# Output projection of a hybrid encoder layer: one pass over all tokens, or two passes over half of them with the first gate and up products behind

## The chip, the cores and the metric

One of the cores of a Trainium2 chip runs the whole program. The metric is the device time of one execution in microseconds. The engines in what follows are TensorE (PE, matmuls), VectorE (DVE), ScalarE (ACT), GpSimd (POOL) and SyncE (SP, which issues most of the DMAs). Each engine works through its own queue in order; they wait for each other through semaphores.

## What is computed

One layer for 560 tokens in float32: 16 meta tokens, 512 prompt tokens and 32 tokens of a running stream. The meta tokens are only keys and values: from the output projection on, 544 tokens count, in two halves of 272.

```python
def layer(h, attend, conv_state, w_in, w_out, conv_w, ...):
    proj = jnp.einsum('btd,de->bte', rms_norm(h, g_pre_mix), w_in)
    q, k, v, gate_b, gate_c, conv_in = jnp.split(proj, SPLITS, axis=-1)
    attn = attend(q, k, v).reshape(b, t, ATTN_WIDTH)
    conv_y, conv_last = short_conv(gate_c * conv_in, conv_state, conv_w)
    mix = jnp.concatenate([group_rms_norm(attn, ...), group_rms_norm(gate_b * conv_y, ...)], axis=-1)
    h = h + rms_norm(jnp.einsum('bte,ed->btd', mix, w_out), g_post_mix)
    xf = rms_norm(h, g_pre_ffn)
    ff = jax.nn.silu(jnp.einsum('btd,df->btf', xf, w_gate)) * jnp.einsum('btd,df->btf', xf, w_up)
    return h + rms_norm(jnp.einsum('btf,fd->btd', ff, w_down), g_post_ffn), k, v, conv_last
```

d_model is 2048 (16 chunks of 128), d_ff 5632 (44 chunks).

## The kernel before

Activations lie with features on the 128 partitions and tokens on the columns. Every float32 operand of a matmul is split into a rounded high part and the low rest, and each product is three matmuls: high x high, high x low, low x high. So a tile of weights is loaded by a DMA, then ACT casts the high part, then DVE subtracts it to get the low part, and then PE can use it.

In the input and the output projection a tile is 8 k-chunks x 128 columns (512 KB). It is loaded into one of two raw buffers (`w_raw`, `load`, L526) and split into one of four slots of `w_hi` and `w_lo` (`round_weights`, L412; `rest_of_weights`, L420). The load of tile t waits until tile t-2 is split; the cast of tile t waits until PE has used tile t-4. Two tiles make the 128 outputs of a chunk. In the output projection there are 16 such chunks, each over all 544 tokens (`two_chunks`, L911, for the first two, which start while the last mix chunks are still being made; `chunk`, L648, for the rest). ACT squares a finished chunk, DVE evacuates it with a gain (L1754), POOL adds up the squares. The loads stand in SP's queue: eight tiles, then waits for the stores of the mixing stage, then the load of the whole residual (4.48 MB, L585), then the other tiles.

When all 16 chunks are there, PE sums the squares over the partitions with matmuls (`row_sums`, L709), ACT makes rstd from them (Ln, Exp, each with its table), DVE scales and adds to the residual (L1763 to L1772), ACT squares the result, PE sums again (L937), ACT makes the second rstd, and DVE normalizes (`normalize`, L1802).

Gate and up projection use a Strassen-like scheme over 2 x 2 blocks: tokens in halves, the contraction in halves of 8 chunks, outputs in pairs of chunks. A step (44 of them, gate and up in turn) has seven products instead of eight, in the order B11, B21, T2, T3, T1, T4, B22 for the weights (`combine`, L1781, makes T1 to T4 on DVE) with A11, A12, S2, S3, S1, A22, S4 for the activations (`xs`; A11 and A12 belong to the first half of the tokens, S1 to S4 are sums and differences of blocks of both halves, made on DVE at L1827 to L1830 and L1914). A product is 8 x 3 = 24 matmuls of 272 columns (`product`, L948). Weights come in panels of 1 MB (`load_panel`, L589); a ring of four tiles (`t_hi`, `t_lo`) holds the split ones. `x_rest` (L1797) splits the activations. The down projection follows with 24 steps of the same kind.

Of the kernel before, what the change touches and what calls it, by code (L numbers as in the profile page):

```python
# [25 lines left out]
P = 128  # L26
# [3 lines left out]
def build_layer(nc, x_prompt, x_sample, cache_k, cache_v, state_conv, meta, w_in, w_out, conv_w,  # L30
# [26 lines left out]
    TK = 8  # L57
# [4 lines left out]
    OUT_T = 2 * KC  # L62
    CH_OUT = IN_T // 2
    CH_FF = CH_OUT + KC
# [56 lines left out]
    with ExitStack() as ctx:  # L121
# [58 lines left out]
        xs = sb_at("xs", 0, [P, 7, 2, KH, TH], F32R)  # L180
# [8 lines left out]
        h2_sq = sb_at("h2_sq", 35840, [P, KC, TL])  # L189
# [5 lines left out]
        hid_hi = sb_at("hid_hi", 201408, [P, 7, TH], F32R)  # L195
        HID_OF = {A11: 1, A12: 2, S2: 5, S3: 0, S1: 4, A22: 3, S4: 6}
# [123 lines left out]
        mix_hi = sem("mix_hi")  # L320
        mix_split = [sem("mix_split0"), sem("mix_split1")]
# [4 lines left out]
        h2_squared = sem("h2_squared")  # L326
        x_normed = sem("x_normed")
# [127 lines left out]

        def panel_of(step, half):
# [29 lines left out]
        def raw_tile(i):  # L486

            step, q = i // 7, i % 7
# [5 lines left out]
        def tile_of(ring, i):  # L494
            return in_tile(ring[:, i % RING_T, :], i // 7)
# [16 lines left out]
        def _(sp):  # L512
# [58 lines left out]
            def load_out(q):  # L571
                at_col = q * 2 * P
                for k in range(4):
                    load((4, q, T_OUT), k, w_out_v[:, TK * (k % 2):TK * (k % 2 + 1),
                                                   bass.ds(at_col + k // 2 * P, P)])
# [10 lines left out]
            for q in range(2, KC // 2):  # L586
                load_out(q)

# [23 lines left out]
            for step in range(1, ALL):  # L612
                if step == 2:
                    sp.wait_ge(xs_lo, 8)
                if step > 2:
                    sp.wait_ge(tile_lo, 7 * (step - 1))
                if step == 1:
                    sp.wait_ge(tile_lo, T1 + 1)
                load_panel(step, 0)
                if step == 1:  # L620
                    sp.wait_ge(xs_lo, 8)
                else:
                    sp.wait_ge(tile_lo, 7 * (step - 1) + T1 + 1)
# [20 lines left out]
        def _(pe):  # L644
# [266 lines left out]
            def two_chunks(tile0, x_wait, lag, between):  # L911


                for c in range(KC + lag):
                    for j, k in ((0, c), (1, c - lag)):
                        if not 0 <= k < KC:
                            continue
                        if k % TK == 0:
                            pe.wait_ge(lo_ready, tile0 + 2 * j + k // TK + 1)
                        if j == 0:  # L920
                            pe.wait_ge(*x_wait(c))
                        mm = multiply(2 * j + k // TK, TK, P, 0, act_hi, act_lo, k // TK * TK, acc_late[j],
                                      [k % TK], k < TK, k >= TK)
                        if k % TK == TK - 1:
                            mm.then_inc((first_used, chunk_done)[k // TK], 1)
                    if c in between:
                        between[c]()

            pe.wait_ge(chunk_copied, CH_OUT)
            two_chunks(T_OUT, mix_chunk, 2, {6: last_norm_and_rows})  # L930
            for q in range(1, KC // 2):
                for c in range(2):
                    chunk((4, q, T_OUT), 2 * c, 2 * q + CH_OUT + c, no_points)
            row_sums(sq_added, sq_made, buf_g[:, LATE], squares[(KC - 1) % 2])


            for g in range(KC // 2):  # L937
                pe.wait_ge(h2_squared, g + 1)
# [1155 lines left out]
```

## Time and profile before

| | us |
|---|---|
| median of three runs | 2453.63 (2452.96 to 2456.07) |
| the profiled execution, its own time | 2450.74 |
| its span in the profile | 2449.0 |
| output projection on PE, steady part | 766 to 934 |
| from its end to the steady gate and up products | 934 to 1022 |

The profile has one execution. Its page gives each engine's busy time and share. [...] The chain of waits is followed back from the last instruction and read forward here: when a piece starts, how long it is, whose it is. Rows of a timeline have start, length, engine, line, operation, output and input, shape, and in brackets how long the engine had been idle and what ended that. Rows of groups have the total and mean length, then the idle time before them. Rows of DMA issues have the count, the size of each, and the median time from issue to landing.

### The profile page before, as it was taken

To read this page: it belongs to the slowest core of one execution; us is meant where nothing else is said; L and a number is where in the kernel's file an instruction comes from. 1 tells how busy PE (TensorE), PEld (TensorE's weight loads), DVE (VectorE), ACT (ScalarE), POOL (GpSimd) and SP (SyncE) were. 2 spreads that over 40 slices of the span, in tenths; PEclk is the share of its full clock that TensorE was granted. 3 is DMA by queue.
4 is the path that set the end of the run, shared out by engine and by line. 5 is a ranking of instruction groups with operands and counts; after the bars stand their busy time and mean duration, and the time that the engine had idled before them with its cause. 6 is when DMAs were issued, how large, how long until landed. Compare 5 with 4: busy or idle time off the path is not lost.

```text
span 2449.0 us, 42232 instructions
## 1 busy us (share of the span) xinstructions
PE 2374.5 (97%) x18280; PEld 2334.6 (95%) x18280; DVE 1541.6 (63%) x1778; ACT 1011.0 (41%) x1245; POOL 81.9 (3%) x143
## 2 busy tenths in 40 slices
PE   8999999999999996699999999999999899999998
PEld 7999999999999995699999999999999899999998
DVE  5323333343434225877777777777777688888887
ACT  6345444432333223444444444444444333333346
POOL 0000000000002110000000000000000000000002
PEclk9999999999999998799999999999999999999999
DMA  7222322222324331234445444444445666645562
GB/s 234 84 75 70 97 77 79 74 87 87 87 81 146 99 104 73 75 130 133 154 135 168 136 154 149 132 155 134 154 134 168 246 210 231 231 143 156 183 204 87
DMA packets 325916, 327.93 MB, mean 134 GB/s; under 512 B 8508, under 2 KB 282324, under 8 KB 325604
## 3 DMA queue, kind: packets, MB, share of 16 engines
q1 hardware_dynamic: 299264, 275.57, 35.9%
q10 hardware_dynamic: 26468, 49.67, 5.5%
q8 instruction: 145, 2.38, 0.4%
q14 instruction: 39, 0.32, 0.0%
HBM read 264.20 MB, written 61.00 MB: 133 GB/s over the span
## 4 chain that ended last, share of the span: by engine, by line
PE 90%; DVE 5%; DMA 2%; ACT 2%; issue 1%; SPq 0%; POOL 0%; ACTq 0%; DVEq 0%; POOLq 0%
PE ps L955 37%; PE ps L438 30%; PE ps L1012 17%; PE ps L722 4%; DMA ff_lo_scr<-hid_lo 2%; PE ps L666 1%; DVE xs L1800 1%; DVE t_lo L1778 1%; DVE misc L1804 0%; DVE panel L1792 0%; DVE wide L1768 0%; DVE misc L1772 0%; ACT xs L1350 0%; DMA panel<-in_w_down_dram 0%; DMA misc<-in_x_sample_dram 0%
## 5 line engine op out<-in xcount | busy, mean ns | idle before, releaser
L955 PE MATMUL ps<-xs,t_hi 128*128 128x272 f32 x4928 | 940.6, 291 | 33.0 <-DVE xs L1800 19.1
L955 PEld LDWEIGHTS ps<-xs,t_hi 128*128 128x128 f32 x4928 | 781.1, 190 | 34.6 <-issue 32.2
L955 PE MATMUL ps<-xs,t_lo 128*128 128x272 f32 x2464 | 716.8, 291 | 0.0
L1778 DVE TENSOR_TENSOR t_lo<-panel,t_hi 128x1024 fp32r<-128x1024 f32 (+1 forms) x405 | 485.5, 1199 | 228.3 <-ACT t_hi L1343 225.3
L1343 ACT CAST t_hi<-panel 128x1024 fp32r<-128x1024 f32 (+1 forms) x405 | 413.4, 1021 | 455.1 <-PE ps L1012 241.9
L1012 PE MATMUL ps<-xd,t_hi 128*128 128x272 f32 x2464 | 470.4, 290 | 14.3 <-DVE y_left L1949 8.2
L955 PEld LDWEIGHTS ps<-xs,t_lo 128*128 128x128 f32 x2464 | 467.3, 190 | 0.0
L438 PE MATMUL ps<-act_hi,w_hi 128*128 128x272 f32 (+1 forms) x2048 | 435.4, 294 | 3.1 <-DVE act_lo L1615 1.9
L438 PE MATMUL ps<-act_lo,w_hi 128*128 128x272 f32 (+1 forms) x2048 | 426.9, 290 | 0.0
L438 PE MATMUL ps<-act_hi,w_lo 128*128 128x272 f32 (+1 forms) x2048 | 426.5, 289 | 0.0
L1012 PEld LDWEIGHTS ps<-xd,t_hi 128*128 128x128 f32 x2464 | 390.7, 190 | 15.5 <-issue 15.4
L1012 PE MATMUL ps<-xd,t_lo 128*128 128x272 f32 x1232 | 358.3, 291 | 0.0
L438 PEld LDWEIGHTS ps<-act_hi,w_hi 128*128 128x128 f32 x2048 | 322.8, 189 | 7.1 <-DVE act_lo L1615 2.6
L438 PEld LDWEIGHTS ps<-act_hi,w_lo 128*128 128x128 f32 x2048 | 324.2, 189 | 0.0
L438 PEld LDWEIGHTS ps<-act_lo,w_hi 128*128 128x128 f32 x2048 | 323.9, 189 | 0.0
L424 DVE TENSOR_TENSOR w_lo<-w_raw,w_hi 128x1024 fp32r<-128x1024 f32 x126 | 157.9, 1254 | 194.8 <-ACT w_hi L418 194.1
L418 ACT CAST w_hi<-w_raw 128x1024 fp32r<-128x1024 f32 x128 | 133.7, 1046 | 281.1 <-PE ps L438 222.4
L1012 PEld LDWEIGHTS ps<-xd,t_lo 128*128 128x128 f32 x1232 | 233.5, 190 | 0.0
L1343 ACT CAST t_hi<-t_raw 128x1024 fp32r<-128x1024 f32 (+1 forms) x68 | 69.7, 1025 | 112.6 <-PE ps L955 69.4
L1381 ACT ACTIVATE m<-ps 128x272 f32<-128x272 f32 x88 | 35.2, 400 | 149.0 <-PE ps L955 149.0
L1549 DVE TENSOR_TENSOR misc<-misc 128x1440 f32<-128x1440 f32 x8 | 13.3, 1658 | 114.3 <-ACT misc L1126 114.3
L1792 DVE TENSOR_TENSOR t_raw<-panel,panel 128x1024 f32<-128x1024 f32 (+1 forms) x67 | 79.3, 1183 | 8.4 <-DMA panel<-in_w_down_dram 6.1
(183 smaller groups left out, 1728.4 us busy)
## 6 DMA issues: line engine op xcount, KB each, us to landing
w_raw<-in_w_in_dram SPq DMA_DIRECT2D x96, 512.0 KB, 3.8
panel<-in_w_up_dram SPq DMA_DIRECT2D x44, 1024.0 KB, 5.6
panel<-in_w_gate_dram SPq DMA_DIRECT2D x43, 1024.0 KB, 5.1
panel<-in_w_down_dram SPq DMA_DIRECT2D x32, 1024.0 KB, 5.9
ff_hi_scr<-hid_hi SPq DMA_DIRECT2D x22, 952.0 KB, 4.5
ff_lo_scr<-hid_lo SPq DMA_DIRECT2D x22, 952.0 KB, 7.4
w_raw<-in_w_out_dram SPq DMA_DIRECT2D x32, 512.0 KB, 3.9
xd<-ff_hi_scr ACTq DMA_DIRECT2D x28, 544.0 KB, 8.0
```

What stands on the lines that cost most here:

```text
L418: nc.scalar.copy(w_hi[:, k % SLOTS, :], raw_slot(k)).then_inc(hi_ready, 1)
L424: engine.tensor_tensor(w_lo[:, k % SLOTS, :], raw_slot(k), w_hi[:, k % SLOTS, :].bitcast(F32), ALU.subtract).then_inc(lo_ready, 1)
L438: mm = nc.tensor.matmul(out[:, h, :], w[:, k, col:col + width], x[:, x_at + k, token + h * half:token + (h + 1) * half], start=begins, sto ...
L666: return nc.tensor.transpose(out, src, ident[0:n, 0:n])
L722: return nc.tensor.matmul(out, w, x, start=start, stop=True, skip_group_check=True)
L955: mm = nc.tensor.matmul(out, w[:, k, :], xs[:, x, part, k, :], start=begins and k == 0 and w is hi and part == 0, stop=k == KH - 1 and w i ...
L1012: mm = nc.tensor.matmul(out[:, n, :], w[:, k, n * P:(n + 1) * P], xd[:, slot, part, k, :], start=q in (B11, B21, T3) and k == 0 and w is h ...
L1343: nc.scalar.copy(tile_of(t_hi, i), raw_tile(i)).then_inc(tile_hi, 1)
L1381: A(out[step % 2][:, :], step_bank(step, letter), ACT.Copy).then_inc(made, 1)
L1778: V.tensor_tensor(tile_of(t_lo, i), raw_tile(i), tile_of(t_hi, i).bitcast(F32), ALU.subtract)\
L1792: V.tensor_tensor(out, x, y, ALU.subtract).then_inc(t_made, 1)
L1800: V.tensor_tensor(xs[:, x, 1, k:k + n, :], block, xs[:, x, 0, k:k + n, :].bitcast(F32), ALU.subtract) .then_inc(xs_lo, 1)
```

## The change

The output projection runs in two passes: first all 16 chunks of outputs for the first half of the tokens, then again for the second half. So a block (the code's e, 0 to 31) is one chunk for 272 tokens, two tiles with 24 matmuls each, and every w_out tile is loaded, cast and split twice. The mix is split into separate tiles for the halves (`mx_hi`, `mx_lo`). Four more tiles, the first ones of gate (two) and up (two), follow through the same raw buffers; PE makes the products B11 and B21 of steps 0 and 1 from them (`pre_product`) behind the second pass, between the sums of the second half's squares. The stage's tail for the first half (scale, add, squares, second rstd, normalization, splits of A11 and A12) is put between the blocks of the second pass on DVE and ACT; its squares are folded on DVE, for one matmul behind block 24. The tail of the second half comes behind the last block, and the sums S1 and S2 get tiles of their own. The stores of the residual go from SP's to ACT's queue.

```diff
-    OUT_T = 2 * KC
+    OUT_T = 4 * KC + 4
...
+        PRE = 4
...
+        def ring(step, q):
+            return 7 * step + q - (2 if step == 0 else PRE)
...
             sp.dma_start(resid, h_scr).then_inc(h_loaded, 16)
-            for q in range(2, KC // 2):
+            for q in range(2, KC):
                 load_out(q)
+            for k in range(PRE):
+                load((4, KC, T_OUT), k, gate_up[k // 2][:, TK * (k % 2):TK * (k % 2 + 1), 0:P])
...
-            for g in range(KC // 2):
-                sp.wait_ge(h2_made, g + 1)
-                sp.dma_start(h_scr[:, 2 * g:2 * g + 2, LATE], resid[:, 2 * g:2 * g + 2, LATE])                  .then_inc(h2_stored, 16)
-
...
+            for e in range(2, 2 * KC):
+                if e >= 4:
+                    pe.wait_ge(out_copied, e - 3)
+                if e == KC:
+                    pe.wait_ge(mix_late, 4)
+                for half in range(2):
+                    pe.wait_ge(lo_ready, T_OUT + 2 * e + half + 1)
+                    out_part(e, half, list(range(TK)))
+                if e == KC:
+                    out_sums(0)
+                if e == KC + 8:
+                    pe.wait_ge(h2_summed, 4)
+                    nc.tensor.matmul(ps[:, 5, 0:TH], neg1[:, :], h2_sq[0][:, 0, :], start=True, stop=True)\
+                        .then_inc(ms_ready, 1)
+            out_sums(1)
...
+            pe.wait_ge(ms_log, 3)
+            pre_product(0)
+            pre_product(1)
+            h2_sums(0)
+            pre_product(2)
+            for g in range(1, 4):
+                h2_sums(g)
+            pre_product(3)
...
+            def square_stream(t, g):
+
+                act.wait_ge(h2_made, 4 * t + g + 1)
+                h = x_block(4 * g, 4, t)
+                A(h2_sq[t][:, 4 * g:4 * g + 4, :], h, ACT.Square).then_inc(h2_squared, 1)
+                act.dma_start(h_scr[:, 4 * g:4 * g + 4, tokens_of(t)], h).then_inc(h2_stored, 16)
+
             act.wait_ge(mixed, end)
...
+            for e in range(2 * KC):
+                t, n, q = e // KC, e % KC, e // 2
+                for half in range(2):
+                    ahead = 2 * e + half + LEAD
+                    if 2 * e + half >= 2 and ahead < OUT_T:
+                        round_weights((4, ahead // 4, T_OUT), ahead % 4)
...
+                A(squares[n % 2][:, t * TH:(t + 1) * TH], ps[:, n % 4, 0:TH], ACT.Square).then_inc(sq_made, 1)
+                if e == KC:
+                    make_rstd(1)
+                if e in (KC + 4, KC + 6):
+                    for g in range(2):
+                        square_stream(0, e - KC - 4 + g)
+                if e == KC + 9:
+                    make_rstd(2)
...
+            for ahead in range(4 * KC + LEAD, OUT_T):
+                round_weights((4, ahead // 4, T_OUT), ahead % 4)
...
+            make_rstd(3)
+            for g in range(4):
+                square_stream(1, g)
+            load_log_table(2)
+            tile_high(ring(0, T2))
+            make_rstd(4)
+            act.wait_ge(product_done, PRE)
+            x_high(A22, x_block(KH, KH, 1), x_normed, 8)
+            x_high(S2, s2_raw[:, :, :], s_made, 2)
...
+            for e in range(2 * KC):
+                t, n = e // KC, e % KC
+                for half in range(2):
+                    ahead = 2 * e + half + LEAD
+                    if 2 * e + half >= 2 and ahead < OUT_T:
+                        rest_of_weights((4, ahead // 4, T_OUT), ahead % 4)
+                if e in (4, 6, 8, 10):
+                    mix_rest_late((e - 4) // 2)
+                dve.wait_ge(sq_made, e + 1)
+                V.tensor_scalar(wide_c[:, n, tokens_of(t)], ps[:, n % 4, 0:TH], column(n + C_POSTMIX), None, ALU.mult)\
+                    .then_inc(out_copied, 1)
+                if e in (KC + 1, KC + 2):
+                    for g in range(2):
+                        scale_mix(0, 2 * (e - KC - 1) + g)
+                if e in (KC + 3, KC + 5):
+                    for g in range(2):
+                        add_mix(0, e - KC - 3 + g)
+                if e == KC + 7:
+                    fold_squares(0)
+                if e == KC + 8:
+                    for level in range(1, 4):
+                        fold_squares(level)
+                if e == KC + 10:
+                    dve.wait_ge(rstd_ready, 3)
+                    dve.wait_ge(h2_stored, 16 * 4)
+                    normalize(0, 0, 4)
+                    normalize(0, 4, 4)
...
-            tile_rest(B11)
+            for g in range(-1, 4):
+                if g + 1 < 4:
+                    scale_mix(1, g + 1)
+                if g >= 0:
+                    add_mix(1, g)
             combine(0, T1)
             combine(0, T2)
             combine(0, T3)
...
+            V.tensor_tensor(s1_raw[:, :, :], a21, a22, ALU.add).then_inc(s_made, 1)
+            dve.wait_ge(product_done, PRE)
+            dve.wait_ge(s_made, 1)
+            V.tensor_tensor(s2_raw[:, :, :], s1_raw[:, :, :], a11, ALU.subtract).then_inc(s_made, 1)
             x_rest(A22, 4, a22)
-            V.tensor_tensor(a22, a21, a22, ALU.add).then_inc(s_made, 1)
             V.tensor_tensor(a21, a11, a21, ALU.subtract).then_inc(s_made, 1)
...
+            x_rest(S2, 5, s2_raw[:, :, :])
+            V.tensor_tensor(a12, a12, s2_raw[:, :, :], ALU.subtract).then_inc(s_made, 1)
```

## Rows read from the trace of the kernel before

**Rows 1.** The page, span and busy time of each engine.
```profile
span 2449.0 us, 42232 instructions
PE 2374.5 (97%) x18280; PEld 2334.6 (95%) x18280; DVE 1541.6 (63%) x1778; ACT 1011.0 (41%) x1245; POOL 81.9 (3%) x143
```
**Rows 2.** The table by stage: out projection, transition, first gate and up steps.
```profile
766.00:934.00 168.00, 168.00 (x1343) 168.00 (x1342) 47.09 (x41) 35.47 (x42) 20.93 (x14) 1.00 0.38 119
934.00:1022.00 88.00, 47.31 (x223) 41.11 (x222) 73.16 (x60) 38.75 (x36) 0.00 (x0) 0.75 0.19 70
1022.00:1140.00 118.00, 118.00 (x925) 118.00 (x925) 90.14 (x101) 54.96 (x71) 0.00 (x0) 0.99 0.42 136
```
**Rows 3.** The chain of waits: start, length, piece.
```profile
934.57 1.91 PE ps L716 x8
...
1001.36 1.14 DVE t_lo L1778
...
1021.78 88.25 PE ps L955 x686
```
**Rows 4.** Groups of PE from 934 to 1022, the gate and up products.
```profile
L955 PE MATMUL ps<-xs,t_hi 128*128 128x272 f32 x98 | 25.7, 361 | 33.0 <-DVE xs L1800 19.1 <-ACT m L1381 11.9 <-DVE gate L1850 2.0
...
L955 PE MATMUL ps<-xs,t_lo 128*128 128x272 f32 x48 | 16.9, 352 | 0.0
```
**Rows 5.** Timeline of ACT: casts of raw tiles, both buffers.
```profile
784.87 1.05 ACT L418 CAST w_hi<-w_raw 128x1024 fp32r<-128x1024 f32 x1 [13.03 <-DMA w_raw<-in_w_out_dram]
...
786.34 1.05 ACT L418 CAST w_hi<-w_raw 128x1024 fp32r<-128x1024 f32 x1
791.16 1.05 ACT L418 CAST w_hi<-w_raw 128x1024 fp32r<-128x1024 f32 x1 [3.77 <-DMA w_raw<-in_w_out_dram]
...
793.97 1.05 ACT L418 CAST w_hi<-w_raw 128x1024 fp32r<-128x1024 f32 x1 [1.24 <-DMA w_raw<-in_w_out_dram]
```
**Rows 6.** Timeline of DVE: last mix chunk's split, a raw tile's split.
```profile
757.43 0.73 DVE L1731 TENSOR_TENSOR act_lo<-wide,act_hi 128x544 fp32r<-128x544 f32 x1 [0.77 <-ACT act_hi L1292]
...
785.96 1.23 DVE L424 TENSOR_TENSOR w_lo<-w_raw,w_hi 128x1024 fp32r<-128x1024 f32 x1 [12.86 <-ACT w_hi L418]
```
**Rows 7.** Timeline of SP's queue: loads of tiles and of the residual.
```profile
766.88 0.37 SPq L531 DMA_DIRECT2D w_raw<-in_w_out_dram  x1
767.68 0.34 SPq L585 DMA_DIRECT2D misc<-h_scratch  x1
768.07 0.42 SPq L531 DMA_DIRECT2D w_raw<-in_w_out_dram  x1
...
787.21 0.37 SPq L531 DMA_DIRECT2D w_raw<-in_w_out_dram  x1
```
**Rows 8.** DMA issues: count, size, median time to landing.
```profile
w_raw<-in_w_out_dram SPq DMA_DIRECT2D x32, 512.0 KB, 3.9
...
misc<-h_scratch SPq DMA_DIRECT2D x1, 4480.0 KB, 15.4
```
**Rows 9.** Timeline of PE behind a gap: pairs of matmuls.
```profile
1002.20 0.79 PE L955 MATMUL ps<-xs,t_hi 128*128 128x272 f32 x2 [9.63 <-ACT m L1381]
...
1008.42 0.41 PE L955 MATMUL ps<-xs,t_hi 128*128 128x272 f32 x2
```
**Rows 10.** Groups of DVE from 934 to 1022, by shape.
```profile
L1804 DVE SCALAR_TENSOR_TENSOR misc<-misc,cols,rstd 128x544 f32<-128x544 f32 x16 | 11.4, 776 | 0.0
L1768 DVE TENSOR_TENSOR wide<-wide,rstd 128x1088 f32<-128x1088 f32 x8 | 10.2, 1284 | 3.2 <-ACT rstd L1094 3.2
...
L1827 DVE TENSOR_TENSOR misc<-misc 128x2176 f32<-128x2176 f32 x1 | 2.4, 2418 | 0.0
```
**Rows 11.** Groups of ACT from 934 to 1022.
```profile
L1331 ACT ACTIVATE h_sq<-misc 128x1088 f32<-128x1088 f32 x8 | 8.9, 1111 | 11.6 <-DVE misc L1772 11.5
...
L1094 ACT ACT_TABLE_LOAD x2 | 2.6, 1283 | 0.0
...
L1087 ACT ACTIVATE rstd<-ps,eps 128x544 f32<-128x544 f32 x2 | 1.4, 714 | 1.6 <-PE ps L716 1.3 <-PE ps L943 0.4
```

More of the change, by code:

```diff
@@ L929, in _ @@
-            pe.wait_ge(chunk_copied, CH_OUT)
[L930 to L938, printed above, removed]
-                for c in (2 * g, 2 * g + 1):
-                    for h, bank in enumerate((bank_a, bank_b)):
-                        if c == 0:
-                            pe.wait_ge(ms_log, 2)
-                        mm = nc.tensor.matmul(bank[:, 0:TH], neg1[:, :], h2_sq[:, c, h * TH:(h + 1) * TH],
-                                              start=c == 0, stop=c == KC - 1)
@@ new lines, in out_sums @@
+            def out_sums(t):
+                for part, (x, added_up) in enumerate(((buf_g[:, tokens_of(t)], (sq_added, (KC - 1) * (t + 1))),
+                                                      (squares[(KC - 1) % 2][:, t * TH:(t + 1) * TH],
+                                                       (sq_made, KC * (t + 1))))):
+                    pe.wait_ge(*added_up)
+                    mm = nc.tensor.matmul(ps[:, 4 + 2 * t, 0:TH], neg1[:, :], x, start=part == 0, stop=part == 1)
+                mm.then_inc(ms_ready, 1)
@@ new lines, in _, with pre_product @@
+            out_sums(1)
+            def pre_product(k):
+                step, q = k // 2, k % 2
+                pe.wait_ge(lo_ready, T_OUT + 4 * KC + k + 1)
+                pe.wait_ge(xs_lo, 3 if q else 2)
+                pe.wait_ge(out_copied, 2 * KC)
+                hi, lo = (w[:, k, :].rearrange("p (k n) -> p k n", k=TK) for w in (w_hi, w_lo))
+                for c in range(KH):
+                    for w, part in ((hi, 0), (hi, 1), (lo, 0)):
+                        mm = nc.tensor.matmul(step_bank(step, "ac"[q]), w[:, c, :], xs[q][:, part, c, :],
+                                              start=c == 0 and w is hi and part == 0, stop=c == KH - 1 and w is lo,
+                                              skip_group_check=True)
+                mm.then_inc(product_done, 1)
@@ new lines, in normalize, with x_rest @@
+            def normalize(t, c0, n):
+                for c in range(c0, c0 + n):
+                    x = resid[:, c, tokens_of(t)]
+                    last = V.scalar_tensor_tensor(out=x, in0=x, scalar=column(c + C_PREFFN), in1=rstd[:, tokens_of(t)],
+                                                  op0=ALU.mult, op1=ALU.mult)
+                last.then_inc(x_normed, 1)
+            def x_rest(x, made, block, k=0, n=KH):
+                dve.wait_ge(xs_hi, made)
+                V.tensor_tensor(xs[x][:, 1, k:k + n, :], block, xs[x][:, 0, k:k + n, :].bitcast(F32), ALU.subtract)\
+                    .then_inc(xs_lo, 1)
@@ L1775, in tile_rest @@
+            for ahead in range(4 * KC + LEAD, OUT_T):
+                rest_of_weights((4, ahead // 4, T_OUT), ahead % 4)
             def tile_rest(i):
@@ L1954, in _ @@
                 step = STEPS + d
-                ahead = 7 * (step + 1)
                 more = step + 1 < ALL
```

373 lines of the change are left out of this document (197 added, 176 removed).

## The prediction

> **What bounds the kernel now.** I read first the busy shares of the page [rows 1]: TensorE (PE) is busy 97% of 2449.0 us, so only its gaps and its pace can give time. Then the table by stage [rows 2]. In the out projection (766 to 934 us) PE is busy in all of 168.00 us with 1343 matmuls: 0.125 us each, so a weight tile of 24 matmuls on 272 columns is 3.00 us. From 934 to 1022 it is busy 47 of 88 us at a granted clock of 0.75, while VectorE (DVE) is busy 73: that is the stage to win in, and it is a DVE chain. The chain of waits says the same: matmul sums at 934.57, then nearly only DVE and ScalarE (ACT) until 1021.78, from where PE runs on [rows 3]. Up to 1022 PE had run 146 matmuls of the gate/up products [rows 4], two of them after 1021.78: 144, or six products. At 24 x 0.126 us a product is worth 3.02 us; so if PE had begun at 1003.7 without a gap it would stand at the same place. After that it still lost some 2 us to pace (925 matmuls in 118.00 us, where 0.125 each is 115.7 [rows 2]). So today's stage works like a clean start at 1005.7, 71 us after the out projection's end at 934.5.
>
> **What the change does to the weights.** Each w_out tile (512 KB) is loaded, cast and split twice, once per half of the tokens: 64 tiles and four gate/up tiles where there were 32. PE's matmuls stay 1536; a tile feeds 24 of them where it fed 48. So PE asks for a tile every 3.00 us, not every 6.0. A tile goes through one of two raw buffers, and the next load into that buffer waits for the split. One round of a buffer stands in the trace where PE was not the limit: cast at 784.87 and again at 791.16 [rows 5], 6.29 us a round: 1.09 from cast to split [rows 6], 1.25 from split to the next load's issue [rows 7], 3.95 from issue to the cast. Two buffers give a tile per 3.15 us. That is more than 3.00: today the buffers have nearly half of PE's time to spare, after the change they set the pace. The other buffer's round there was 7.63 (786.34 to 793.97 [rows 5]), with an evacuation between: I take 6.29, and 6.00 (PE's own pace) and 7.6 are the bounds.
> [...] The trace's median for these loads, issued from SyncE (SP), is 3.9 us [rows 8], and I go by it.
>
> **Start of the first pass.** The load of the residual (4.48 MB, 15.4 us [rows 8]) stands in SP's queue behind the first eight tiles. The tile load behind it, issued at 768.07 [rows 7], could be cast only at 784.87, after a wait of 13.03 [rows 5]: 16.8 us after issue. Today PE has four tiles of 6 us in hand and does not notice. In the new order the first two blocks end some 1.5 us after the last mix chunk is split (757.43 [rows 6], a little earlier with half the width): 758.8. ACT can round tile 5 only behind the square of block 0: cast, split, the next load at 761.3, the residual's load 0.8 later and tile 8's at 762.5, with the spacing of [rows 7]. It is usable at 762.5 + 16.8 + 1.1 + 1.2 = 781.6. PE ran out of tiles at 758.8 + 12.0 = 770.8: **a stall of 10.8 us**. [...]
>
> **The two passes.** From tile 8 the even buffer gives tile 48 after 20 rounds: 781.6 + 125.8 = 907.4. The odd buffer follows 2.8 us later at first. DVE and ACT get more work between its rounds as of block 16: scale and add on 1088 columns (1.28 us each, 1.20 apart), two 1.11 us squares and two store issues on ACT, table loads of 1.28 [rows 10, 11]. A round leaves DVE 6.3 - 2 x 1.2 - 0.4 = 3.4 us, so pieces of 2.4 fit once the odd tiles have slid to some 4.6 us behind the even ones. With 0.8 us for the stores: tile 49 at 912.7 and block 24 (0 is the first) done at 915.7.
> **The fold.** Behind block 24 PE's queue has a wait for four sums of squares that DVE folds, and three of its four folds come after block 24's own evacuation. ACT must first round tiles 51 and 52 (tile 52 lands at 918.8), so: cast to 919.9, square, split of 52 to 921.1, evacuation to 921.5, folds of 1088, 544 and 272 columns 2.6 us, one matmul: 924.4. **PE stands 8.7 us**, and every tile behind it in PE's queue stands too. If ACT were ahead it would be 3.7 (square 0.4, evacuation 0.4, folds 2.6, matmul 0.3). [...]
> Fourteen tiles of 3.00 follow: **the out projection ends at 924.4 + 2.5 + 42.0 = 968.9, 34.4 us later than today**.
>
> **The new transition.** The last gate/up tile's load is issued when tile 65 is split (970.1) and lands at 974.1; its cast on ACT stands ahead of the second half's rstd: 1.05, Ln 0.4, table 1.28, Exp 0.4 (half of [rows 11]): R = 977.2. From R: eight half operations of 1.2 (9.7); the last square, its store's issue, a table load with its activation, the cast of T2's tile and the second rstd on ACT: R + 16.2; 16 normalizations of 272 columns, 0.41 each (0.78 on 544 with 0.70 apart [rows 10], half plus the fixed part): R + 22.9; two sums of 2176 (2.35 apart) and then three more such operations, the last the split of S2: T2 of step 0 starts at R + 34.7. From the split of S2 to the last product of step 0 it takes 20.4 us today (1001.36 to 1021.78 [rows 3]), now 19.2, since the split of step 1's first tile is gone; four more DVE operations to T2 of step 1: R + 57.9 = 1035.1. By then nine products are done, four of them early (27.2 us), in PE time that DVE's chain leaves free anyway. The clean start is at 1007.9.
> **Sum:** 1007.9 against 1005.7 is +2.2 us: the stage itself falls from 71 to 39 us and gives 32, and the passes take 34.4 of it back. The profiled execution took 2450.74 us (span 2449.0); the median of three is 2453.63, and I add to that: **2456 us**. The four early products, half 0's norm and the panel loads behind SP's queue (5 us each, landing before R) are costed at nothing because DVE's chain covers them. Should the early products find no cover, they cost 12 us. The steps and the down projection keep their order and lengths.
>
> **The rivals.**
> A, the forecast: 2456, itself 2451 to 2462 by the steps' own slack (the fold's wait, the odd buffer's slide, half pace).
> B, PE sets the pace: a load lands in 3.6 us or less and rounds run ahead. Then block 24 ends at 781.6 + 2.8 + 126 = 910.4, the fold costs 3.7 and 1.5 of pace, the end is 957.6, and R comes 3.7 us after it, since tile 67 is there: clean start at 992.0, 13.7 us faster: 2440. For it: rows of 3.9 are only 0.3 us from the point where 6.29 turns to 6.00. Against it: that 6.29 is what the row shows where nothing else held the buffer.
> C, the slower side: DVE's and ACT's inserted work pushes both buffers' rounds, not the odd one's alone. The place is blocks 16 to 30, and it decides as soon as an insertion is over the 3.4 us that a round leaves. With a mean round of 7.0 us, halfway to 7.63, it is 15 x 0.7 = 10.5 us: 2466. For it: the row of 7.63, with one evacuation alone. Against it: that round caught up at once.
> D, the change doesn't do what it says: half 0's norm is not through by the end of pass two and the early products come behind the DVE chain, 12 us: 2468.
>
> **How the numbers follow.** A 0.46, B 0.25, C 0.20, D 0.09. About 0.2% (4.9 us) is what a measurement here can tell from no change: 2448.7 to 2458.5. A lies in it with 0.33 and above it with 0.13; B below with 0.24 and 0.01 inside; C above with 0.18 and 0.02 inside; D above. So faster 0.24, same 0.36, slower 0.40. A alone is the likeliest and it crosses the bound. The range goes from just above B's time to just above D's: 2441 to 2469.
>
> **What would show it.** In the profile after: PE without work for some 11 us near 771 to 782, with the cast of tile 8 waiting for a DMA; ACT's casts of w_raw waiting for the DMA and not for PE, with 6.3 us between every second one; a wait of 4 to 9 us of PE for DVE some 50 us ahead of the out projection's end; that end near 969; T2 of step 0 some 43 us after it. I am wrong if the casts wait for PE (B), if rounds in pass two are 7 us (C), or if the end of the projection is before 958.

## The result: slower by 13.8 us, with the profile after

| | before | after |
|---|---|---|
| median of the timed runs | 2453.63 us (2452.96 to 2456.07) | 2467.40 us (2466.70 to 2469.87) |
| ratio to before, 95% interval | | 1.0058 [1.0046, 1.0069] |
| the profiled execution, its span | 2450.74, 2449.0 | 2467.40, 2465.7 |

The forecast was 2456 in 2441 to 2469: the time is in the range, 11.4 us above the forecast, and on the side that had the chance 0.40.

The page of after, against [rows 1]: PE has the same busy time, so the loss is in gaps again.

```profile
span 2465.7 us, 42439 instructions
PE 2374.8 (96%) x18250; PEld 2332.2 (95%) x18250; DVE 1587.8 (64%) x1851; ACT 1051.7 (43%) x1306; POOL 96.0 (4%) x158
```

The table by stage of after, with the stretches of [rows 2] (the stretch and its length; busy us, and in brackets the instructions, of PE, PE's weight loads, DVE, ACT, POOL; PE's granted clock as a share of full speed, DMA share, GB/s):

```profile
766.00:934.00 168.00, 140.28 (x1045) 135.22 (x1044) 87.97 (x86) 66.41 (x82) 29.97 (x22) 0.94 0.60 172
934.00:1022.00 88.00, 63.75 (x452) 61.22 (x452) 66.59 (x74) 44.89 (x49) 8.29 (x6) 0.88 0.40 122
1022.00:1140.00 118.00, 113.25 (x859) 112.46 (x859) 92.63 (x98) 55.11 (x70) 0.00 (x0) 0.96 0.40 132
```

Of the first 168 us PE now lacks 27.7, where it lacked none. In the middle stretch it has 452 matmuls instead of 223, but a part of these are the out projection, which ends there. In the last it has 859 against 925. The clean start of the sum (where PE would have to begin gate and up without a gap) is found as before: step 1's block T2, from which PE runs on, begins at 1044.71, and nine products of 3.02 us stand ahead of it: 1017.5. For before, six products ahead of 1021.78 give 1003.7. The difference is 13.8 us, as much as that of the medians.

The two profiled executions differ by 16.7 us. The other 3 are at the end of the program, which the change does not touch: the same 177 matmuls had a granted clock of 1.00 in before's execution and 0.86 in after's. In an execution of the kernel before with one more buffer (an experiment below) it was 0.81. So I put it down to the execution, not to the change; one execution of each kernel was profiled. The three rows are before, after, and that kernel:

```profile
2426.00:2449.00 23.00, 19.36 (x177) 18.64 (x176) 14.32 (x20) 13.75 (x24) 0.00 (x0) 1.00 0.55 195
```
```profile
2439.40:2465.70 26.30, 22.54 (x177) 21.62 (x176) 14.78 (x20) 13.98 (x24) 0.00 (x0) 0.86 0.47 171
```
```profile
2425.00:2452.00 27.00, 24.11 (x177) 23.17 (x177) 14.77 (x20) 14.15 (x24) 0.00 (x0) 0.81 0.46 166
```

Now the stage itself, in three places. The DMA issues of after, to set beside [rows 8]:

```profile
w_raw<-in_w_out_dram SPq DMA_DIRECT2D x64, 512.0 KB, 4.0
...
misc<-h_scratch SPq DMA_DIRECT2D x1, 4480.0 KB, 15.1
```

**The passes.** ACT's timeline of after, the casts of raw tiles behind the start (in brackets: idle before it, and what ended it), to set beside [rows 5]:

```profile
773.62 1.04 ACT L429 CAST w_hi<-w_raw 128x1024 fp32r<-128x1024 f32 x1 [11.56 <-DMA w_raw<-in_w_out_dram]
...
787.11 1.05 ACT L429 CAST w_hi<-w_raw 128x1024 fp32r<-128x1024 f32 x1 [3.67 <-DMA w_raw<-in_w_out_dram]
```

The line of these casts in after from 782 to 918 us, as a group:

```profile
L429 ACT CAST w_hi<-w_raw x40: 1035/1048/1059, 782.4 to 917.0; 128x1024 fp32r<-128x1024 f32 x40
...
  DMA w_raw<-in_w_out_dram: 77.9, 38
```

The same line in before, from 766 to 934 us:

```profile
L418 ACT CAST w_hi<-w_raw x26: 1040/1047/1052, 765.5 to 911.1; 128x1024 fp32r<-128x1024 f32 x26
...
  PE ps L438: 40.5, 9
  DMA w_raw<-in_w_out_dram: 24.2, 5
```

In before 9 of the 26 casts waited for PE and 5 for a load; after the change 38 of 40 wait for a load, and none is put down to PE. 40 casts from 782.4 to 917.0 are 39 steps of 3.45 us: PE gets a tile every 3.45 us, where it can use one every 3.00. From PE's side, its timeline around the stall at tile 8, 9.7 us from the start of one matmul to the start of the next:

```profile
766.36 0.28 PE L947 MATMUL ps<-mx_hi,w_lo 128*128 128x272 f32 x1
776.07 0.57 PE L947 MATMUL ps<-mx_hi,w_hi 128*128 128x272 f32 x1 [9.42 <-DVE w_lo L435]
```

**The fold.** The chain of waits of after around it (start, length, piece):

```profile
909.44 7.51 DMA w_raw<-in_w_out_dram
...
916.97 1.06 ACT w_hi L429
...
918.05 1.24 DVE w_lo L435
...
919.30 3.90 DMA w_raw<-in_w_out_dram
...
925.52 0.41 DVE wide L1907
925.94 1.36 DVE h_sq L1880
```

And PE's timeline at that place:

```profile
917.91 0.28 PE L947 MATMUL ps<-mx_hi,w_lo 128*128 128x272 f32 x1
928.58 1.27 PE L988 MATMUL ps<-h_sq,neg 128*128 128x272 f32 x2 [10.39 <-DVE h_sq L1880]
```

Two tiles have to land, be cast and be split before DVE comes to the folds: PE's wait of 10.4 us is named after DVE, but the chain that leads to it goes through loads of 7.5 and 3.9 us.

**The transition.** The chain of waits of after, from the projection's end (973.7, where the second of the two matmuls that sum its squares starts; the ends of other runs are read at the same matmul) to the first product that needs the second half:

```profile
973.10 2.50 DVE xs L1892
975.60 1.14 DVE w_lo L435
...
976.76 3.85 DMA w_raw<-in_w_up_dram
...
980.64 1.05 ACT w_hi L429
...
983.38 0.44 ACT rstd L1173
...
993.86 5.51 PE ps L1012 x24
...
1001.20 0.44 ACT rstd L1173
...
1001.67 6.70 DVE misc L1885 x16
```

PE's timeline behind the early products (the last one, and what it then waits for):

```profile
1002.10 0.29 PE L1002 MATMUL ps<-xs,w_lo 128*128 128x272 f32 x1
1020.50 0.79 PE L1031 MATMUL ps<-xs,t_hi 128*128 128x272 f32 x2 [18.11 <-DVE xs L1892]
```

### The profile page after: what moved, and what is told of

Read it like the earlier page. It is cut to its first block, busy times and chain, and to the rows that moved or that the text cites. A ratio compares the mean times of both kernels' runs of the same rounds, so it can differ in the third digit from the quotient of the medians.

```text
span 2465.7 us, 42439 instructions
## 1 busy us (share of the span) xinstructions
PE 2374.8 (96%) x18250; PEld 2332.2 (95%) x18250; DVE 1587.8 (64%) x1851; ACT 1051.7 (43%) x1306; POOL 96.0 (4%) x158
## 4 chain that ended last, share of the span: by engine, by line
PE 83%; DMA 7%; DVE 5%; ACT 3%; issue 1%; SPq 0%; ACTq 0%; POOLq 0%; POOL 0%; DVEq 0%
PE ps L1031 36%; PE ps L449 23%; PE ps L1090 17%; DMA w_raw<-in_w_out_dram 5%; PE ps L748 4%; DVE w_lo L435 2%; PE ps L692 2%; DMA ff_lo_scr<-hid_lo 2%; ACT w_hi L429 1%; DVE xs L1892 1%; PE ps L947 0%; PE ps L1012 0%; DVE t_lo L1941 0%; DVE misc L1885 0%; DMA misc<-in_x_sample_dram 0%
## 5 line engine op out<-in xcount | busy, mean ns | idle before, releaser
L1090 PEld LDWEIGHTS ps<-xd,t_hi 128*128 128x128 f32 x2464 | 390.2, 190 | 15.6 <-issue 15.6
L449 PE MATMUL ps<-act_hi,w_hi 128*128 128x280 f32 (+1 forms) x1536 | 328.9, 295 | 2.1 <-DVE act_lo L1717 1.8
L449 PE MATMUL ps<-act_lo,w_hi 128*128 128x280 f32 (+1 forms) x1536 | 320.7, 290 | 0.0
L449 PE MATMUL ps<-act_hi,w_lo 128*128 128x280 f32 (+1 forms) x1536 | 320.7, 290 | 0.0
L449 PEld LDWEIGHTS ps<-act_hi,w_hi 128*128 128x128 f32 x1536 | 242.3, 188 | 5.9 <-DVE act_lo L1717 2.5
L449 PEld LDWEIGHTS ps<-act_hi,w_lo 128*128 128x128 f32 x1536 | 243.3, 189 | 0.0
L449 PEld LDWEIGHTS ps<-act_lo,w_hi 128*128 128x128 f32 x1536 | 243.0, 189 | 0.0
L947 PE MATMUL ps<-mx_hi,w_hi 128*128 128x272 f32 x512 | 153.0, 299 | 18.7 <-DVE w_lo L435 17.4
L947 PE MATMUL ps<-mx_lo,w_hi 128*128 128x272 f32 x512 | 149.2, 291 | 0.0
L947 PE MATMUL ps<-mx_hi,w_lo 128*128 128x272 f32 x512 | 148.6, 290 | 0.0
L947 PEld LDWEIGHTS ps<-mx_hi,w_hi 128*128 128x128 f32 x512 | 98.2, 192 | 23.9 <-issue 16.0
```

The lines of the kernel that those rows point to most:

```text
L449: mm = nc.tensor.matmul(out[:, h, :], w[:, k, col:col + width], x[:, x_at + k, token + h * half:token + (h + 1) * half], start=begins, sto ...
L947: mm = nc.tensor.matmul(ps[:, n % 4, 0:TH], w[:, k, :], x, start=c == 0 and w is hi and part == 0, stop=c == KC - 1 and w is lo, skip_grou ...
L1090: mm = nc.tensor.matmul(out[:, n, :], w[:, k, n * P:(n + 1) * P], xd[:, slot, part, k, :], start=q in (B11, B21, T3) and k == 0 and w is h ...
```

## Experiments

**The theory.** The two raw buffers set the pace of both passes, and what sets a round of a buffer is the landing of its load. The four early products cost nothing. **The rivals:** the work of the first half's norm, put between the rounds on DVE and ACT, sets it (C); PE's wait at the fold is the loss; SP's queue, in which the residual's load stands, is the loss; or the early products lie in the path (D). All runs are compared with the kernel before on the same chip (medians of 2453.5 to 2454.0 us there); differences from the change itself are taken from its 2467.40.

### A third raw buffer

A third buffer serves from tile 8 of the out projection on; a load waits for the split three tiles back instead of two (`behind` is t - 3).

```diff
+        w_raw2 = sb_at("w_raw2", 130048, [P, TK * P])
...
-                    sp.wait_ge(lo_ready, t - 1)
...
+                    sp.wait_ge(lo_ready, behind + 1)
```

> The changed kernel with a third raw buffer (4 KB a partition, in room that the mixing stage has left) as of the ninth output tile. Theory 1, two raw buffers set the pace: a round of 6.3 to 6.8 us over three buffers is under 2.3 us a tile, PE's 3.0 us rule; block 24 ends some 130 us after tile 8 instead of 142, the fold's wait shrinks from 10.7 to about 4 us, the second half's rstd comes about 5 us after the projection's end instead of 10: 2445 us, give or take 4. Theory 2, the work put between the blocks on DVE and ACT sets the pace: another buffer changes nothing in their order, rounds of a tile pair stay at 6.8 us: 2464 or more.

Measured: 2442.06 us, ratio 0.9948 [0.9932, 0.9965]: 25 us faster than the change, some 11.5 faster than before. The stall at tile 8 stays (9.75 us). The same line of casts in the same stretch:

```profile
L440 ACT CAST w_hi<-w_raw x43: 1031/1049/1061, 784.3 to 916.0; 128x1024 fp32r<-128x1024 f32 x43
...
  PE ps L961: 33.8, 16
  DMA w_raw<-in_w_out_dram: 8.7, 5
```

The casts now wait for PE in 16 cases and for a load in 5. At the fold PE is idle for 4.3 us (4.6 from the start of its last matmul, at 906.05); the projection ends at 955.0 and the second half's rstd follows 3.4 us later, at 958.40. These numbers are close to those of rival B (957.6, and 3.7 behind it), and so is the time (2440): B had the right working for the case in which the buffers don't bind.

### The wait at the fold, later

PE's wait for the folded squares stands behind block 26 instead of block 24; rstd, normalization and splits of the first half one block later.

```diff
-                if e == KC + 8:
+                if e == KC + 10:
                     pe.wait_ge(h2_summed, 4)
```

> The changed kernel with PE's wait for the folded squares behind block 26 instead of 24; the rstd, normalization and splits of the first half that hang on it come one block later. Theory 1, the wait costs PE time: the gap of 10.7 us near 918 is gone, PE goes on at the buffers' pace (3.4 us a tile, 14 tiles), the projection ends some 8 us sooner: 2459 us. Rival: the buffers run ahead in the wait and PE makes up for it behind it, so it is nearly free: 2465 to 2468.

Measured: 2462.56 us, ratio 1.0038 [1.0023, 1.0053], 4.8 below the change. The wait of 10.4 us is gone; the projection ends at 971.3 instead of 973.7, in an execution that issued its first load 1.9 us later (708.66 against 706.80). Neither expectation was met in full: of the 10.4 us and the slow pace behind them some 5 came back, and the rest is taken by the loads. The casts' group of this run:

```profile
L429 ACT CAST w_hi<-w_raw x40: 1031/1049/1055, 781.9 to 915.8; 128x1024 fp32r<-128x1024 f32 x40
...
  DMA w_raw<-in_w_out_dram: 79.6, 37
```

That is 39 steps of 3.43 us: the pace of the change itself. The fold is a loss of its own, and the smaller one.

### Half of each load

From tile 8 on a load brings only four of the tile's eight chunks of rows, so half of the weights are left out; cast, split and matmuls stay as they are.

```diff
+                if t >= T_OUT + 8:
+                    dst, src = dst[:, 0:TK // 2], src[:, 0:TK // 2]
```

> The changed kernel, but as of the ninth output tile a load brings only the first four of a tile's eight k-chunks (256 KB); the rest of the buffer keeps old data, so part of the weights is left out. Casts, splits, matmuls, waits and their order stay. Theory 1, the round is set by the load: it lands at least 0.6 us sooner, a round falls to 6.0 us or under and PE sets the pace: 2445 to 2455. Theory 2, ACT's and DVE's queues set the round: rounds stay near 6.8: 2464 or more.

Measured: 2445.47 us, ratio 0.9962 [0.9947, 0.9977]. The line of the DMA issues (count, size, median us to landing), then the casts' group:

```profile
w_raw<-in_w_out_dram SPq DMA_DIRECT2D x56, 256.0 KB, 2.7
```
```profile
L429 ACT CAST w_hi<-w_raw x43: 1031/1053/1058, 783.8 to 915.9; 128x1024 fp32r<-128x1024 f32 x43
...
  PE ps L949: 26.5, 14
  DMA w_raw<-in_w_out_dram: 16.3, 14
```

DVE and ACT have exactly the work of the change, two buffers as there, and the pace is nearly that of three buffers: 42 steps of 3.15 us, the wait at the fold (3.7 us here) included. So the queues of DVE and ACT do not set the rounds by themselves. A shorter landing would, however, hide a small insertion as well; whether C's insertions lengthen the rounds is read from the trace of the change. On the even buffer, from tile 10 to tile 48, a round is 6.67 us on the mean: 4.32 of landing and 2.36 of everything else, the same 2.36 in pass one, which has nothing of the first half's norm in it, and in pass two. The prediction's row had 3.95 and 2.34. On the odd buffer everything else grows from 2.58 us in pass one to 2.82 in pass two: the insertions cost the odd buffer 0.24 us a round there and the even one nothing. So C falls, and the landing is what is longer. C's time, 2466, was right by coincidence.

### The residual's load on ACT's queue

```diff
-            sp.dma_start(resid, h_scr).then_inc(h_loaded, 16)
+                if e == 1:
+                    act.dma_start(resid, h_scr).then_inc(h_loaded, 16)
```

> The changed kernel with the load of the residual issued from ACT's queue behind block 1 instead of from SP's queue between the tile loads. Theory 1, the ninth tile's load waits behind the residual in one queue: it now lands in 5 to 8 us instead of 16.5, the gap of 9.7 us near 770 falls to under 3, and with it everything behind it, less what the two transfers take from each other: 2457 to 2461 us. Rival, the transfer itself fills the DMA engines: the tile lands as late as before: 2465 to 2468.

Measured: 2467.12 us, ratio 1.0056 [1.0041, 1.0071]: no gain, and my first theory of this run falls. The timeline, SP's queue first, then ACT's issue and the next cast:

```profile
756.03 1.50 SPq L560 DMA_DIRECT2D w_raw<-in_w_out_dram  x2
```
```profile
755.18 0.36 ACTq L1426 DMA_DIRECT2D misc<-h_scratch  x1
...
771.42 1.04 ACT L429 CAST w_hi<-w_raw 128x1024 fp32r<-128x1024 f32 x1 [15.37 <-DMA w_raw<-in_w_out_dram]
```

The residual is issued ahead of the eighth tile's load here. That load, issued on SP at 756.03, behind nothing in SP's queue, could be cast only at 771.42, after the 4.48 MB issued on ACT at 755.18 had landed (14.6 us after issue); the ninth tile's, issued at 757.16, landed 15.7 us after issue. A queue of its own did not help these two loads past this transfer. The DMA queues of this run from 761 to 767 us (packets, MB, share of the 16 engines' time; q10 is ACT's queue, q1 SP's) show what happens:

```profile
q10 hardware_dynamic: 73, 2.62, 101.3%
q1 hardware_dynamic: 72, 0.04, 2.0%
```

The two queues ran as many packets as each other, 73 and 72 in these 6 us. But in the trace a packet of the residual is 35,840 bytes and takes 1.33 us, and a packet of a tile load is 512 bytes and takes 0.03 us. Over 16 engines the 72 small packets are one per engine every 1.33 us (16 x 6 / 72), the length of a large one: by 767 us only 78 of the 2,048 packets of the two tile loads had run.

### The early products, cut short

Each of the four is made of 3 matmuls instead of 24; most of their contraction is left out.

```diff
-                for c in range(KH):
+                for c in range(1):
...
```

> Each of the four early products is made of 3 matmuls instead of 24, so most of their contraction is left out; the rounding of their tiles, the normalization, the x splits and all waits stay. Theory (the early products lie beside DVE's and ACT's chain of the second half's normalization, which sets the restart): the idle stretch of PE ahead of the step-0 block that needs the second half (18.4 us in the changed kernel, 1002.10 to 1020.50) grows by what the products shrink, the restart stays within 1 us of 1020.5 and the time stays 2467 within 1.5. Rival (products are in the chain, by the pace PE restarts at or by the tiles they hold): the restart comes earlier, and the time falls by 4 us or more, up to 9.

Measured: 2471.03 us (2465.01 to 2471.60), ratio 1.0065 [1.0050, 1.0080]: not faster, and 2.5 us above what the theory gave. The projection ended 2.3 us later in the profiled execution (975.97 against 973.70), so the chain is read from its own start. In the change the first rstd behind the projection ends at 983.82, the second 17.8 us later and PE restarts 36.7 after it; here it is 985.97, 18.2 and 37.0. The chain of waits shows why even the sums gain nothing:

```profile
990.89 4.00 PE ps L1012 x8
994.88 0.68 PE ps L1002 x3
995.56 6.31 PE ps L1012 x24
```

With the product between them gone the sums start 0.5 us earlier after rstd, but their 24 matmuls take 6.31 us instead of 5.51: PE had been idle for 6.4 us just before 990.89, and went on at a lower pace: its granted clock from 990 to 1002 us was 0.71, where the change has 1.00 from 988 to 1002. The early products cost the chain nothing.

### The early products, made late

The reverse: the same four products behind the second half's sums and normalization.

```diff
             pe.wait_ge(ms_log, 3)
-            pre_product(0)
...
-            for g in range(1, 4):
+            for g in range(4):
                 h2_sums(g)
-            pre_product(3)
+            pe.wait_ge(x_normed, 8)
+            for k in range(PRE):
+                pre_product(k)
```

> The four early products are made from the same tiles, but behind the second half's sums and its normalization instead of ahead of them, so that nothing covers them. Theory (as made in the change they lie in time that DVE's chain takes anyway): the restart of PE behind them moves from the second rstd + 18.9 us to the second rstd + 29 to 34: the products' own 12 us (four of 24 records of 0.126 us, three times each) at full or partly half pace, less the 2.4 us of the first sum that DVE makes meanwhile; the time goes to 2477 to 2482. Rival (the products cost the chain as much as they save, since the sums of the squares wait for one of them): second rstd 3 us earlier, and the time at most 2473.

Measured: 2483.04 us, ratio 1.0119 [1.0104, 1.0134], 15.6 above the change and 1 us above what the theory expected. The chain of waits:

```profile
1011.72 13.95 PE ps L1002 x96
```

The second rstd comes 17.9 us after the first, as in the change, so the rival falls. From it to PE's restart (1035.27) it is 30.3 us instead of 18.9: the cover is worth 11.4 us on the path. In this execution the first rstd itself was 3.3 us later; the projection had already ended 3.2 us later, ahead of everything that the edit touches.

### The residual in pieces

The 4.48 MB come in eight transfers of two chunks, one ahead of every fourth tile load from tile 8 on (the code's q counts loads by four, so that q is 2 to 9 where the blocks are 4 to 19); two raw buffers.

```diff
-            sp.dma_start(resid, h_scr).then_inc(h_loaded, 16)
             for q in range(2, KC):
+                if q < 10:
+                    c = 2 * (q - 2)
+                    sp.dma_start(resid[:, c:c + 2, :], h_scr[:, c:c + 2, :]).then_inc(h_loaded, 16)
                 load_out(q)
...
```

> Two raw buffers as in the changed kernel; the 4.48 MB residual comes in 8 transfers of two chunks (0.56 MB), one ahead of the four tile loads of each of blocks 2 to 9, instead of in one. Theory 1 (the loop of a raw buffer has no slack: whatever the DMA engines carry beside a tile load is added to its landing): the stall of 9.7 us at tile 8 goes, but each piece adds up to 1.9 us (15.1 us for 4.48 MB, an eighth) to one tile's landing in four; 8 times 1.0 to 1.9 is 8 to 15 us, so the time stays at 2462 to 2470. Theory 2 (a piece goes through in the 2.3 us of each round in which its buffer's engine works and no load is under way): the stall goes and little comes back, 2458 within 2.

Measured: 2461.99 us (2460.65 to 2464.07), ratio 1.0035 [1.0022, 1.0047], 5.4 below the change. The stall of 9.7 us is gone. Of the early casts of this run the one that waits longest waits 4.74 us, where it was 11.56:

```profile
764.05 1.05 ACT L429 CAST w_hi<-w_raw 128x1024 fp32r<-128x1024 f32 x1 [4.74 <-DMA w_raw<-in_w_out_dram]
```

Theory 1 gave 2462 to 2470, theory 2 2456 to 2460: the time stands at the lower end of the first, but the trace does not show the price that theory 1 puts on a piece. Tiles 12 to 33, beside which pieces run, land in 4.24 us on the mean, and in 4.26 in the change. The profiled execution issued its first load of the projection 3.5 us later than that of the change (710.26 against 706.80), ahead of everything that the edit touches; counted from there, the matmul behind the fold (924.02 against 928.58) comes 8.0 us earlier, and the projection's end 7.9. So some 2 us of the 9.7 come back by this execution and some 4 by the medians, 0.2 to 0.5 us a piece and not the 1.0 to 1.9 that I had put down. A second thing changed with the cut: a packet of a piece has 4,480 bytes where one of the whole residual has 35,840. Which of the two helps, the spreading or the smaller packets, was not parted.

### Third buffer and later fold; with the pieces; with three moves behind the projection

> Third raw buffer (as in the run with it alone, 2442.06) and, beside it, PE's wait for the folded squares two blocks later with the work behind it one block later. If PE sets the pace with three buffers, PE's time at that wait (4.6 us from 906.05 in the run with the third buffer) is all lost time: the gap falls to what the eviction wait needs (under 1 us) and the time to 2438, within 1.5. If the remaining gap is instead made up again behind it (the tiles run ahead in the meantime and PE was to wait for a tile anyway), the time stays at 2442 within 1.

Measured: 2439.63 us, ratio 0.9941 [0.9926, 0.9956]: 2.4 below the third buffer alone, less than the 4.3 us that PE was idle there, more than nothing.

> The run with everything (2428.73) without its three moves behind the projection; it parts their gain from that of the residual's 8 pieces. If the pieces take the stall of 9.7 us away and hide beside three buffers, it gives 2430 within 1.5 (2439.63 less 9.7) and the moves are worth 1 to 2 us; if the pieces give back a third or more, 2433 or above, and the moves are worth 4 or more.

Measured: 2426.72 us (2424.40 to 2431.25), ratio 0.9892 [0.9878, 0.9907]. That is 12.9 below the run without the pieces, more than the stall of 9.7, and below both expectations. The first stretch of its table by stage:

```profile
766.00:934.00 168.00, 166.81 (x1327) 166.17 (x1326) 112.53 (x120) 84.87 (x104) 26.10 (x27) 1.00 0.75 217
```

PE is busy 166.8 of 168 us at the full clock, with a DMA share of 0.75 against 0.60 in the change: what PE lost in the first stretch is regained.

> Third raw buffer, the later wait for the folded squares, the residual in 8 pieces, and three moves behind the projection: the logarithm's table loaded a block earlier, the second half's rstd ahead of the rounding of the early products' last tiles on ACT, its first scaling ahead of the last remainders on DVE. With three buffers PE sets the pace and tile loads have slack, so the pieces hide: from 2438 the stall of 9.7 us at tile 8 falls away, and the three moves take some 2 to 4 us out of the 18.4 us in which PE waits behind the projection: 2426, within 4. If the pieces cost what they save with three buffers too, 2436.

The edit beside those: the logarithm's table one block earlier, the second half's rstd on ACT ahead of the last cast, its first scaling on DVE ahead of the last split. Measured: 2428.73 us (2427.02 to 2429.69), ratio 0.9897 [0.9882, 0.9912]. It lies in the expected range, but the run without the three moves shows that they bring nothing that can be measured.

### The kernel before with the third buffer

> The kernel before with the third raw buffer in its out projection, the control for the run that gave 2442.06 with it. Theory (the buffers bind only where each tile serves half the tokens, and in the kernel before the idle PE time stands at the norm behind the projection): no change, 2453.5 within 2, so that the two passes are worth 11 us once the buffers no longer bind. Rival (the third buffer speeds any out projection): 2447 or less, and the two passes are worth 5 us or nothing.

Measured: 2454.36 us, ratio 1.0001 [0.9992, 1.0011]. The same edit that takes 25 us off the change does nothing to before. Its first stretch is that of [rows 2]:

```profile
766.00:934.00 168.00, 168.00 (x1343) 168.00 (x1342) 47.75 (x41) 35.96 (x42) 20.39 (x14) 1.00 0.39 119
```

So on equal terms (three buffers on both sides) the two passes are worth 12.3 us (2454.36 to 2442.06). With the fold and the residual's pieces mended it is 27.6; before was not run with the pieces, but its PE is busy in all of this stretch and has no stall that they could take away. The change was a gain behind a bound that it brought with it.

## Why the prediction was right in its order and wrong by 11 us

By its own steps; each number on the left is the prediction's.

- **The round of a buffer, 6.29 us: the mechanism was right, the term mis-sized.** It was read from one round [rows 5] with a landing of 3.95. The even buffer took 6.6 us a round in pass one (787.11 to 853.17, 10 rounds) and 6.7 from there to block 24 (853.17 to 907.10, 8 rounds); the odd one took 6.8 and 6.9. That is close to the 7 us in pass two that I had named as the sign of C, but pass one, without C's insertions, is nearly as long. The median landing is 4.0, hardly above the 3.9 of [rows 8], but the mean of the 56 loads behind the stall is 4.3 us, since 11 of them took over 4.7 and the longest 7.51, beside two stores of the residual on ACT's queue at 907.2 and 907.7. A loop without slack pays the mean, and I had priced it at a good round: 20 rounds at 6.67 instead of 6.29 are 7.6 us. Block 24 ended at 918.2, where the start's gain of 5.5 us (next point) taken off 915.7 gives 910.2: 8 us. That it is the bound was right: with three buffers, or with half loads, it is gone.
- **The stall at tile 8, 10.8 us: right in size (9.70), 5.5 us early.** PE ran dry at 766.4, not 770.8, and had tile 8 at 776.1, not 781.6. The last mix chunk that the first half needs was split at 751.72, 5.7 us before the 757.43 that I had started from with "a little earlier". The reason that I gave for the stall was not the whole one: off SP's queue the 4.48 MB held the tile loads up as much (15.4 and 15.7 us).
- **The fold, 8.7 us: 10.4.** The chain is the predicted one link by link, up to the second load (3.90) and the folds (1.36, 0.74, 0.45). The surplus is again a landing: 7.51 us ahead of the cast of tile 50, behind which tile 52's load waits. The split between passes and fold is that of one execution: in the two runs on the early products, with the same code up to there, block 24 ended 5.3 and 5.5 us later and PE waited 7.5 and 6.9 us.
- **The rest of the projection behind the fold, 44.5 us (2.5 of it slow pace): 45.1.** It ends at 973.7 where I had 968.9.
- **The terms for slow pace (2.5 us in 924.4 + 2.5 + 42.0; in B 2.8 behind the stall and 1.5 behind the fold):** no run shows them at these places. What the runs showed there is a granted clock of 0.50 for a shorter time. The rows are before behind its gap of 9.63 us [rows 9], then after behind the stall and behind the fold:

```profile
1002.20:1008.42 6.22, 6.22 (x27) 6.22 (x28) 6.22 (x5) 4.05 (x5) 0.00 (x0) 0.50 0.05 8
```
```profile
776.07:778.90 2.83, 2.83 (x12) 2.83 (x13) 1.55 (x2) 0.07 (x1) 0.47 (x1) 0.50 0.55 155
928.58:932.40 3.82, 3.82 (x15) 3.59 (x16) 1.08 (x1) 0.00 (x0) 0.00 (x0) 0.50 0.44 128
```

At 0.126 us a matmul there is room for 49, 22 and 30, so 2.8, 1.3 and 1.9 us were lost (an estimate from these rows).

- **End to rstd, 8.3 us: 10.1.** One DVE operation was left out: the rest of x for A12 (2.50 us at 973.10) stands ahead of the split that releases the last load. With three buffers the tile is there already, and it is 3.4.
- **rstd to T2, 34.7: 36.7,** 1.6 of it the sums of squares (5.51 us on PE behind the third early product, which I had at the pace of DVE's squares). T2 of step 1: 57.9 predicted, 60.9 measured.
- **The early products at nothing: right,** shown from both sides (short: no gain; late: 11.4 us on the path, where I had said 12). D falls. The panel loads too: the second one landed at 988.0, after rstd and not before as I wrote, but it is first used at 994.8.
- **The 2 us of slow pace that I added to before's clean start (1003.7 to 1005.7): a mistake.** After has it too. The table of after from its own clean stretch on:

```profile
1045.00:1140.00 95.00, 95.00 (x744) 95.00 (x743) 72.80 (x82) 42.92 (x56) 0.00 (x0) 0.98 0.40 131
```

744 matmuls in 95.00 us are 0.128 each, and before's 925 in 118.00 [rows 2] are 0.128. The loss lies in the first 6 us behind the clean restart, at a granted clock of 0.72 in both executions. So it belongs on both sides of the sum or on neither. In the executions of two other runs (the later fold, and before with the third buffer) the clock is 1.00 there (from 1042 to 1048 and from 1022 to 1028 us) and the loss is absent: 47 and 46 matmuls in these 6 us, where after has 38 from 1045 to 1051 and before 37 from 1022 to 1028.

The sum of these: start -5.5, passes +8.0, fold +1.7, the rest of the projection +0.6, its end to T2 of step 1 +4.8, the pace that I credited +2.0. That is +11.6, the whole miss of the stage (13.8 measured against 2.2).

The chances were put well on the sign that came (0.40), though for the wrong reason: C and D, which carried more than half of it, both fell. What came was A's mechanism, by a landing time with a tail, but 5 us above the 2462 at which A's own range ended. That the time is still in the stated range is owed to the room left for D.

## What to carry to other kernels

When a change halves the work that a transfer feeds, compare the round of a buffer with the new pace first (here 6.67 us against 6.00), and price it with the mean of the landings and their tail (4.3 us, the longest 7.51), not with a median or a good round (4.0, 3.95); a buffer of 4 KB a partition turned 13.8 us of loss into 11.5 of gain here. For the large transfer beside this loop, pieces that were spread took 5.4 us off the time, and another queue 0.3, less than a measurement here can tell; look at the size of its packets too (35,840 bytes beside 512). And an expected gain that doesn't come may still be there: add the missing resource to both kernels, and see what the change is worth on equal terms.

## What was not expected of the hardware

A 0.5 MB load on SP's queue, issued 0.85 us after a 4.48 MB load on ACT's queue, took 15.4 us, as long as the large one; the median of these loads in the change is 4.0. From 761 to 767 us the two queues ran 73 and 72 packets, but one's packets were 35,840 bytes and the other's 512. Halving a load from 512 to 256 KB took its median landing from 4.0 to 2.7 us. And the same 177 matmuls at the end of the program had granted clocks from 0.81 to 1.00 in different executions, 3 us of the time.

## What stays open

Why single loads take 5 to 7.5 us was not taken apart by a run. In the trace of the change three of the 11 loads over 4.7 us, the longest among them, run beside the stores of the first half's residual. And during 9 of the 11 a packet of 8 or 16 KB of the queues that the profile calls instruction was under way, during 14 of the other 45. Neither was moved in any run, so no cause is shown. And of the 12.9 us that the pieces bring with three buffers 3 are more than the stall they remove; that run's own spread (2424.40 to 2431.25) is of that size.
